# The first block's gate columns and bonus sums in other places of the instruction streams

## The reference, cut to what matters

```python
h = rmsnorm(x, norm_mix_pre)
proj = h @ w_in        # q, k, v, rw (3360 columns), gate_a, gate_b (1024 columns each)
y_att = sliding_window_attention(q, k, v, att_sinks) @ w_o_att
y_rw = rwkv7_time_mix(rw, ...) @ w_o_rw
mixed = jax.nn.sigmoid(gate_a) * y_att + jax.nn.sigmoid(gate_b) * y_rw
...
# inside rwkv7_time_mix, behind the scan over the tokens:
y = ((y - mean) * lax.rsqrt(var + GN_EPS)).reshape(B, S, RW_DIM) * gn_w + gn_b
bonus = jnp.sum(rh * kh * r_k, axis=-1, keepdims=True) * vh
out = (y + bonus.reshape(B, S, RW_DIM)) * g
```

## Time and profile before

| | |
|---|---|
| three runs | 4483.31, 4487.18, 4489.5 us, median 4487.18 |
| profiled execution | 4486.73 us, of which the profile's span is 4485.0 |
| PE busy | 4140.2 us, 92% |
| DVE, ACT, POOL busy | 44%, 34%, 13% |
| attention's steps, first layer and second | from 106 to 216 us, and from 1445 to 1554 us |
| recurrence's operands | from 262 to 457 us, and up to about 1795 us |
| behind the scan, to the last gate column | about 690 to 757 us, and about 2025 to 2091 us |

### The profile page before, as it was taken

How to read it: one execution, slowest core, us unless ns; L and a number is a source line. 1 busy time by engine, 2 the same in 40 slices (tenths; PEclk the granted TensorE clock), 3 DMA queues, 4 the chain that set the end, 5 groups by cost and what they waited for, 6 DMA issues and landing times.

```text
span 4485.0 us, 74524 instructions
## 1 busy us (share of the span) xinstructions
PE 4140.2 (92%) x32508; PEld 3240.5 (72%) x32508; DVE 1956.2 (44%) x2973; ACT 1513.7 (34%) x2697; POOL 578.6 (13%) x408
## 2 busy tenths in 40 slices
PE   7899789899998999779899989987899999999999
PEld 5676776677776776776677767755688888667877
DVE  5536335455335536435455344357432232444232
ACT  3533233333333533333333333257221121343221
POOL 1215101011002216100011001012000000150000
PEclk9999899899998999999899999999999999999999
DMA  4122002244323132003244321100111111101222
GB/s 161 39 101 74 31 4 104 80 169 169 138 83 105 43 107 67 32 16 110 90 169 169 130 78 43 52 24 1 38 62 62 62 66 57 57 6 66 94 94 85
DMA packets 97684, 351.74 MB, mean 78 GB/s; under 512 B 10064, under 2 KB 13648, under 8 KB 95952
## 3 DMA queue, kind: packets, MB, share of 16 engines
q1 hardware_dynamic: 86480, 313.02, 20.3%
q10 hardware_dynamic: 10880, 33.96, 2.1%
HBM read 332.26 MB, written 14.68 MB: 77 GB/s over the span
## 4 chain that ended last, share of the span: by engine, by line
PE 81%; DVE 8%; issue 4%; POOL 3%; ACT 3%; ACTq 0%; DMA 0%; DVEq 0%; POOLq 0%; SPq 0%
PE ps L350 20%; PE ps L351 20%; PE ps L353 20%; PE ps L1376 7%; PE ps L2418 1%; PE ps L1936 1%; DVE sml L2493 1%; DVE wlo L307 1%; POOL e L2952 1%; ACT whi L297 1%; PE ps L391 1%; POOL dd L1218 1%; PE ps L2865 1%; DVE x L521 1%; POOL ops L1226 1%
## 5 line engine op out<-in xcount | busy, mean ns | idle before, releaser
L307 DVE TENSOR_TENSOR wlo<-ring,whi 128x1024 fp32r<-128x1024 f32 x494 | 624.4, 1265 | 1828.5 <-ACT whi L297 1828.2
L297 ACT CAST whi<-ring 128x1024 fp32r<-128x1024 f32 x494 | 517.6, 1048 | 2071.0 <-PE ps L353 1793.4
L350 PE MATMUL ps<-h_hi,whi 128*128 128x512 f32 x1424 | 596.8, 419 | 22.3 <-DVE h_lo L461 10.2
L351 PE MATMUL ps<-h_lo,whi 128*128 128x512 f32 x1424 | 569.1, 400 | 0.0
L353 PE MATMUL ps<-h_hi,wlo 128*128 128x512 f32 x1424 | 568.3, 399 | 0.0
L350 PE MATMUL ps<-hm_hi,whi 128*128 128x512 f32 (+1 forms) x1408 | 514.3, 365 | 16.0 <-DVE hm_lo L464 14.6
L351 PE MATMUL ps<-hm_lo,whi 128*128 128x512 f32 (+1 forms) x1408 | 480.5, 357 | 0.0
L353 PE MATMUL ps<-hm_hi,wlo 128*128 128x512 f32 (+1 forms) x1408 | 418.6, 355 | 0.0
L350 PEld LDWEIGHTS ps<-h_hi,whi 128*128 128x128 f32 x1424 | 272.4, 191 | 142.4 <-issue 48.7
L350 PE MATMUL ps<-ac_hi,whi 128*128 128x512 f32 x880 | 330.6, 376 | 3.0 <-DVE wlo L307 3.0
L350 PEld LDWEIGHTS ps<-hm_hi,whi 128*128 128x128 f32 x1408 | 267.0, 190 | 85.8 <-DVE hm_lo L464 19.3
(11 more groups left out here) (386 smaller groups left out, 7161.2 us busy)
## 6 DMA issues: line engine op xcount, KB each, us to landing
ring<-in_w SPq DMA_DIRECT2D x590, 512.0 KB, 3.3
h_spill<-h ACTq DMA_DIRECT2D x2, 2048.0 KB, 6.7
x_spill<-x ACTq DMA_DIRECT2D x2, 2048.0 KB, 13.8
m_spill<-m ACTq DMA_DIRECT2D x2, 2048.0 KB, 9.2
h_again<-h_spill ACTq DMA_DIRECT2D x2, 2048.0 KB, 8.7
ma<-m_spill ACTq DMA_DIRECT2D x2, 2048.0 KB, 10.4
x<-x_spill ACTq DMA_DIRECT2D x2, 2048.0 KB, 9.9
x<-in_x SPq DMA_DIRECT2D x4, 512.0 KB, 7.5
```

Of the source, the lines that this page charges most:

```text
L297: self.A.copy(self.hi[k % 2][:], raw).then_inc(self.s_cut_hi.h, 1)
L307: self.V.tensor_tensor(self.lo[k % 2][:], raw, self.hi[k % 2][:].bitcast(F32), ALU.subtract).then_inc(self.s_cut_lo.h, 1)
L350: T.matmul(ps[:, b, 0:cw], hi, xh(q, c0, cw), start=q == 0, stop=False, skip_group_check=True)
L351: T.matmul(ps[:, b, 0:cw], hi, xl(q, c0, cw), start=False, stop=False, skip_group_check=True)
```

## The change

In the attention the sixteen half columns stand in it = 0 to 18 without 4, 8 and 12, on PE, ACT and DVE, and the cast of a group's outputs (L952) comes after the gate copy and the piece's cast. In the recurrence's operands bonus j moves from behind column first[j] + 2 into the middle of column first[j] + 3, ahead of its fifth step, and DVE's reading of it moves to the tick of that column; the last one (j = 7) stands behind column 26, ahead of the scan. Behind the scan the columns 4 and 6 of gate_b go to bank 6, a column from 5 on waits for the gate two columns back, and DVE norms the first tile of a pair before the low parts of the previous pair.

```diff
@@ dense @@
-                    self.column(steps, xh, xl, segs, banks_of(n), ready if n == 0 else None)
+                    self.column(steps, xh, xl, segs, banks_of(n), ready if n == 0 else between(n) if between else None)
@@ window_attention @@
+        gate_at = {it: i for i, it in enumerate(it for it in range(N + 3) if it not in (4, 8, 12))}
...
                 if it < N:
                     pe_scores(it)
-                if it >= 3:
-                    pe_gate(it - 3)
+                if it in gate_at:
+                    pe_gate(gate_at[it])
...
-                    if n == 3:
-                        A.wait_ge(self.s_oc.h, b_oc + j + 1)
-                        A.copy(o_hi[:, 2 * g:2 * g + 2, :], o_[:, 2 * g:2 * g + 2, :]).then_inc(self.s_hhi.h, 1)
-                    act_gate(j)
+                if it in gate_at:
+                    act_gate(gate_at[it])
+                if it >= 3 and n == 3:
+                    A.wait_ge(self.s_oc.h, b_oc + j + 1)
+                    A.copy(o_hi[:, 2 * g:2 * g + 2, :], o_[:, 2 * g:2 * g + 2, :]).then_inc(self.s_hhi.h, 1)
...
-                if it >= 3:
-                    dve_gate(it - 3)
-                    if steps[it - 3][0] == 3:
-                        dve_low(steps[it - 3][1])
+                if it in gate_at:
+                    dve_gate(gate_at[it])
+                if it >= 3 and steps[it - 3][0] == 3:
+                    dve_low(steps[it - 3][1])
@@ recurrence_operands @@
-        at_bonus = {n + 2: j for j, n in enumerate(first)}
+        at_bonus = {n + 3: j for j, n in enumerate(first)}
...
-            if n in at_bonus:
+            if n >= N and n in at_bonus:
                 pe_bonus(at_bonus[n])
+
+        def between(n):
+            return (lambda q: pe_bonus(at_bonus[n]) if q == 4 else None) if n in at_bonus else None
@@ recurrence_out @@
+        def gate_bank(n):
+            return 6 if n > 3 and n % 2 == 0 else 7
...
-                if n > 0:
+                if n > 4:
+                    T.wait_ge(self.s_gate.h, b_gate + n - 1)
+                elif 0 < n < 4:
                     T.wait_ge(self.s_gate.h, b_gate + n)
...
         def dve_gate(n, value):
+            if n in outs:
+                dve_norm(outs[n][0])
             for j in outs.get(n - 1, ()):
...
-            for j in outs.get(n, ()):
-                dve_norm(j)
+            if n in outs:
+                dve_norm(outs[n][1])
```

More of the change, by code:

```diff
@@ L560, in dense @@
     def dense(self, cols, xh, xl, segs, banks_of, free, ready=None, pe_tick=None, act_tick=None,
-              dve_tick=None, pool_tick=None, paired=False, hold=None):
+              dve_tick=None, pool_tick=None, paired=False, hold=None, between=None):
         first = cols[0][0].cut
@@ L1250, in recurrence_operands @@
         go(*self.dense(cols, hh, hl, SEG1, lambda n: [n % 3], free, None, pe_tick, act_tick, dve_tick, pool_tick,
-                       hold=cols[-1][-1].cut))
+                       hold=cols[-1][-1].cut, between=between))
         for n in range(N, max(at_bonus) + 1):
@@ L1746, in pe_gate @@
             for n, steps in enumerate(cols):
-                if n > 0:
+                if n > 4:
+                    T.wait_ge(self.s_gate.h, b_gate + n - 1)
+                elif 0 < n < 4:
                     T.wait_ge(self.s_gate.h, b_gate + n)
                 self.column(steps, lambda q, c0, cw: h_hi[:, q, c0:c0 + cw], lambda q, c0, cw: h_lo[:, q, c0:c0 + cw],
-                            SEG1, [7], (lambda q: T.wait_ge(self.s_hlo.h, b_hlo + q + 1)) if n == 0 else None)
+                            SEG1, [gate_bank(n)], (lambda q: T.wait_ge(self.s_hlo.h, b_hlo + q + 1)) if n == 0 else None)
                 for j in sums.get(n, ()):
@@ L1766, in act_gate @@
             A.wait_ge(self.s_mm.h, value)
-            A.activation(GB[:, n, :], ps[:, 7, :], ACT.Sigmoid).then_inc(self.s_gate.h, 1)
+            A.activation(GB[:, n, :], ps[:, gate_bank(n), :], ACT.Sigmoid).then_inc(self.s_gate.h, 1)
             for j in means.get(n, ()):
@@ L1854, in free_y @@
                 T.wait_ge(self.s_ynorm.h, b_norm + DT)
-            if n == 3:
-                T.wait_ge(self.s_gate.h, b_gate + DT)
+            if n in (2, 3):
+                T.wait_ge(self.s_gate.h, b_gate + DT - 3 + n)
             if n >= 4:
```

## The result

The changed kernel takes 4511.1 us (median of four runs, 4507.83 to 4519.37) against 4488.3 us for the kernel before on the same chip: ratio 1.0058, 95% interval 1.0046 to 1.0069, so 21 to 31 us slower. 4513 us was forecast, in a range of 4492 to 4522. The profiled execution took 4511.18 us, its span 4509.5.

What follows compares the result with a forecast made beforehand. The prediction took ACT and DVE to be as tight as PE in the attention, and POOL and DVE to set the bonus lap. Its terms, +3 + 29.2 - 5.5 = +26.7 us on 4486.7, gave 4513 us, range 4492 to 4522.

Steps and rivals of the forecast that it cites:

- The bonus: Recurrence's operands: odd bonuses wait for the previous reading, lengthening laps and delaying the scan; +29.2 us, bounds +17 and +31.
- The wait foreseen at 7.3 us: In the middle of column 21, PE waits from 409.7 to 417.0 us for DVE's reading of bonus 2.
- The clock's 2.0 us: Twelve matmuls behind each long bonus wait run slow at a lower clock: 2.0 us for each of three laps per layer.
- The three delays: Laps of bonuses 1, 3 and 5 grow by 1.6, 2.4 and 2.4 us, plus 2.0 us each for the clock.
- PE's old wait: The 2.55 us wait ahead of every odd bonus; claimed hidden, since POOL and DVE set the lap.
- The second rival: Bonus: the reading isn't late and PE sets the lap; 26.7 us gained in both layers, 4457 us; chance 0.10.
- The attention: Half columns from the first iteration on, in both layers: +3 us, bounds -14 and +9.
- The step through the iterations: Attention's 19 iterations stepped through with traced durations of PE, ACT, DVE and POOL: -0.5 and +0.3 us.
- a lower clock behind the two long waits: Attention: slow matmuls behind the waits in it = 8 and 12; one and a half us per layer may reach the loop.
- four waits of the transposes: Attention: PE waits 1.8, 1.2, 3.7 and 4.9 us in it = 4, 5, 8 and 12.
- the copies' new order: Attention's end: gate copy and piece come 0.95 us sooner, taking away the 1.0 us wait for the low part.
- Behind the scan: The norm before two low parts removes three 0.9 us waits per layer, the second bank nothing: -5.5 us, bounds -6.4 and 0.

Runs made afterwards that it cites:

- e4: The changed kernel with DVE's reading of the bonus moved to the head of its tick, ahead of its wait for dd: 4473.3 us, 0.9969 of the kernel before.
- e10: The kernel before with only the bonus's part of the change, and DVE's reading of the bonus first in its tick: 4478.8 us against 4485.9, 0.9984.
- e6: The kernel before with each bonus one column later, at that column's end, DVE's reading still behind the shift: 4486.8 us, 0.9995.
- e5: The kernel before with DVE's reading of bonus sums 0 to 4 ahead of its wait for dd, the bonus's matmul unmoved: 4487.2 us against 4487.7, 0.9999.
- e1: The kernel before with the attention's part of the change alone (half columns and order of copies): 4491.9 us against 4487.0, 1.0011.
- e7: The kernel before with only ACT's copies to o_hi put behind the gate copy and casts: 4479.5 us against 4487.7, 0.9984.
- e9: The kernel before with the attention's part alone, and DVE's subtraction for o_lo one step later: 4483.7 us, 0.9989 of the kernel before.
- e11: The changed kernel with DVE's reading of the bonus first and the o_lo subtraction one step later: 4469.6 us, 0.9964 of the kernel before.
- e8: The kernel before with only the norm ahead of the low parts, gate's columns all on bank 7: 4482.2 us against 4485.9, 0.9984.

## Why the prediction was right, and where its terms were off

**The bonus: right, in its parts too.** Forecast +29.2 us, measured alone +26 (21 to 32); the rows give +31.8 for the stage up to the scan's first product with `bar`, a little over the +31 that was named as the upper bound. The most that the clock was to cost behind a wait, 2.3 us, has no working in the prediction: by its own 2.8 us for twelve matmuls at full clock, half clock would cost as much again. The wait foreseen at 7.3 us is 5.9 to 8.0 us. The clock's 2.0 us for the half column behind it is 5.3 - 3.3 = 2.0. The three delays, forecast as 3.6, 8.0 and 12.4 us, can be read off dd of columns 18, 21 and 24: 395.88, 419.84 and 443.97 us before, 403.89, 431.76 and 460.90 after; less the 3.8 us by which the stage began late they are 4.2, 8.1 and 13.1. The scan's first product with `bar` has then 2.9 us more (forecast 2.2). That the reading of the previous bonus is the cause was a claim; e4 and e10 show it by taking the reading forward, e6 by letting the matmul come later. That PE's old wait was hidden behind POOL and DVE, as the prediction had it, is shown by the laps of e5 and e6. It had PE's low clock hidden too, and that holds: PE was busy 21.4 us in a lap before against 20.0 at a granted clock of 1.00 in e10, and the lap did not follow it; the change put such slow matmuls on the path.

**The second rival**, PE sets the lap, put the turning point where it is (the reading must be done by the middle of the column). e4 and e10 come near to that by another order: the reading ends 1.7 to 2.8 us late instead of 5.9 to 8.0. The rival priced it at 26.7 us in both layers; the stages gave back 8.0, because the lap of POOL and DVE, 22.9 us, comes next.

**The attention: the sign right, but by luck.** Forecast +3, measured +5 (1 to 9). The step through the iterations gave -0.2 us in both layers; the rest of the forecast was 3 us for a lower clock behind the two long waits. The traces show it the other way round. PE's idle time grew by 3.4 us in the first layer and 3.3 in the second; its busy time, where a lower clock would stand, changed by +0.3 and +1.6 us, and in e1 by -1.5 and +0.2. So it was the waits that cost the time, not the clock. The length of the attention was to stay within 3 us and grew by 3.7 and 4.9. The step through the iterations forecast four waits of the transposes, 1.8, 1.2, 3.7 and 4.9 us, 11.6 in all. The first layer shows 0.73, 0.91, 3.81 and 5.14, and one of 1.47 in step 16, 12.0 in all. What was off is the rest of PE's idle time. In the first layer's attention it was 13.5 us before (109.6 - 96.07), and a gain of 0.5 us leaves 13.0, of which 11.6 were those four; so 1.4 us remained for the waits on the gate copy, which are 4.9:

```profile
106.40:216.00 109.60, 96.07 (x657) 73.85 (x657) 67.92 (x155) 59.56 (x194) 26.91 (x16) 0.94 0.12 39
1445.20:1553.90 108.70, 94.35 (x656) 72.23 (x656) 67.92 (x155) 59.45 (x194) 26.91 (x16) 0.95 0.12 40
```

(kernel before) and after it

```profile
106.30:219.60 113.30, 96.36 (x656) 73.82 (x656) 67.78 (x155) 59.35 (x194) 26.89 (x16) 0.94 0.12 38
1457.40:1571.05 113.65, 95.98 (x656) 73.36 (x657) 67.56 (x155) 59.47 (x194) 26.90 (x16) 0.94 0.11 38
```

The idle time of the first layer is 16.9 us now: the term that the step had too small is the wait for the gate copy. Against that, the copies' new order was priced at the 1.0 us at the end of each layer, while e7 shows 7 us in both. So the half columns themselves cost 12 us, where the forecast leaves 5 for them (3 and the two times 1.0). The mechanism named for step 12, small terms behind a group's cast and low part, is borne out by e9's time and by e11's trace: with the low part later the wait there is 0.84 us instead of 5.14, though 2.03 us come back in step 13. In step 8, where the prediction named POOL and ACT's copy, the same edit leaves 2.67 of 3.81 us.

**Behind the scan: right.** Forecast -5.5 us with nothing for the second bank, measured -6 (2 to 10), and e8 has it without the bank. By the two profiles the stretch from the scan's end to the first y column is 3.6 and 3.5 us shorter, of which the waits are 2.7.

## What to carry to other kernels

A wait in a list says who came last at that point, not what sets the pace: before moving a step to remove one, find the engines that wait only for each other around the loop (here POOL and DVE), and look for the instruction that stands in the answer of one to the other. When two users share one buffer, moving the writer forward or back is only half an edit: the reader's place in its own queue has to move too, ahead of the wait that it does not need; here these two lines were the difference between 23 us lost and 14 gained. And work that is moved from steady steps into a loop's start leaves holes behind it: step through them as carefully as through the place where it goes.

## What the runs showed of the hardware

The length of a POOL operation depends on what DVE does beside it. The subtraction dd takes 1.04 us while DVE idles, and 2.02 in the kernel before at 419.84 us, where it lies beside this one:

```profile
418.93 2.03 DVE L307 TENSOR_TENSOR wlo<-ring,whi 128x1024 fp32r<-128x1024 f32 x1 [0.21 <-ACT whi L297]
```

In e10's laps every dd takes 1.04 us, and the multiply by k_f, which has the whole of DVE's subtraction for the weights' low part beside it, 2.81 instead of 1.68:

```profile
414.75 2.81 POOL L1237 TENSOR_TENSOR ops<-ops,k_f 128x512 f32<-128x512 f32 x1 [1.98 <-DVE k_f L1166]
417.52 1.04 POOL L1221 TENSOR_TENSOR dd<-zb 128x512 f32<-128x512 f32 x1
```

DVE's subtraction itself takes 1.23 us where POOL is idle. Beside POOL's multiplies it is not always the one that is drawn out: at 400.66 it takes 2.30 us, and at 415.19, beside the multiply of 2.81, it takes 1.21:

```profile
400.66 2.30 DVE L307 TENSOR_TENSOR wlo<-ring,whi 128x1024 fp32r<-128x1024 f32 x1
...
415.19 1.21 DVE L307 TENSOR_TENSOR wlo<-ring,whi 128x1024 fp32r<-128x1024 f32 x1
```

The Trainium skill, "GPSIMD Engine Reference", key points, states that GpSimd shares its SBUF interfaces with VectorE and that instructions of VectorE with two SBUF inputs contend; these rows agree, and put 1.0 us on dd and 1.1 on the multiply. What decides which of the two engines is held up is not worked out here. A lap of these two engines can't be summed from the durations of each alone.

PE's granted clock does not follow its idle time in the lap alone: 2.5 us of idle a lap went with 0.93 before, 2.9 us with 1.00 in e10, and 6.5 us with 0.86 after the change. In e5 two laps in a row have 3.1 us of idle at 1.00 and 1.5 us at 0.93. Full speed is the level of 2.4 GHz. The runs don't settle what makes the difference.
